# Expert products of 512 columns, gate/up one block ahead of down, in a hybrid Mamba and mixture-of-experts layer

## The reference

```
xb  = xt[tok]                                     # gather the block's tokens
gu  = xb @ w_gate_up[e] + b_gate_up[e]            # 1024 -> 2048
glu = min(gu[:, :1024], 7);  lin = clip(gu[:, 1024:], -7, 7)
act = glu * sigmoid(1.702 * glu) * (lin + 1)
yb  = (act @ w_down[e] + b_down[e]) * g[:, None]  # 1024 -> 1024
out[tok] += yb
```

## Time and profile before

| | us |
|---|---|
| median of 3 runs | 1605.25 (1603.05 to 1607.25) |
| the profiled execution | 1617.12 |
| its span, first to last instruction | 1615.5 |
| experts, first to last expert matmul | 538.4 to 1586.5 |
| TensorE busy | 1518.4 (94% of the span) |
| weight loads busy | 1282.4 (79%) |
| VectorE busy | 605.4 (37%) |
| 384 transfers of 1 MB, median from issue to landing | 12.7 |

### The profile page before, as it was taken

How to read it: one execution, slowest core, us unless ns; L and a number is a source line. 1 busy time by engine, 2 the same in 40 slices (tenths; PEclk the granted TensorE clock), 3 DMA queues, 4 the chain that set the end, 5 groups by cost and what they waited for, 6 DMA issues and landing times.

```text
span 1615.5 us, 50223 instructions
## 1 busy us (share of the span) xinstructions
PE 1518.4 (94%) x21227; PEld 1282.4 (79%) x21227; DVE 605.4 (37%) x1324; ACT 297.4 (18%) x449; POOL 380.3 (24%) x511
## 2 busy tenths in 40 slices
PE   6898999999995699999999999999999999999994
PEld 4897889875453367799989888889997898999883
DVE  4666988865024222322232222232232223232223
ACT  5442333342021001110110110011011011011102
POOL 1000000000003323233323333232324232333332
PEclk8998999999997799999999999999999999999997
DMA  3222222142446599999999999999999999999983
GB/s 117 78 79 104 105 104 104 56 178 104 197 156 178 202 404 403 398 406 406 406 397 405 404 403 397 403 401 408 402 396 407 405 402 398 407 404 408 395 310 120
DMA packets 88777, 478.79 MB, mean 296 GB/s; under 512 B 16374, under 2 KB 29178, under 8 KB 34610
## 3 DMA queue, kind: packets, MB, share of 16 engines
q1 hardware_dynamic: 65266, 456.94, 70.1%
q0 software_dynamic: 23488, 21.55, 6.7%
HBM read 463.66 MB, written 19.07 MB: 299 GB/s over the span
## 4 chain that ended last, share of the span: by engine, by line
PE 64%; issue 2%; DMA 1%; DVE 1%; POOL 0%; ACT 0%; POOLq 0%; ACTq 0%; DVEq 0%; SPq 0%
PE bank L1399 64%; DMA expert_sum<-moe_f,idx_now 0%; DMA ring<-expert_sum 0%; DMA moe_f<-n_scratch,idx_next 0%; DVE reg_x L1158 0%; DVE reg_b L1146 0%; DVE reg_b L1158 0%; DVE reg_x L1146 0%; POOL slot_table L490 0%; POOL expert_sum L524 0%; DMA idx_raw<-slot_table 0%; POOL idx_raw L504 0%; ACT reg_a L740 0%; DVE moe_f L1095 0%; ACT moe_f L733 0%
## 5 line engine op out<-in xcount | busy, mean ns | idle before, releaser
L1399 PE MATMUL bank<-ring,moe_f 128*32 128x256 f32 x18432 | 1029.9, 380 | 30.6 <-issue 17.4
L1399 PEld LDWEIGHTS bank<-ring,moe_f 128*32 128x32 f32 x18432 | 905.2, 110 | 155.3 <-issue 65.7
L1118 DVE STREAM_TRANSPOSE moe_f<-bank 128x384 f32<-128x384 f32 x64 | 37.3, 583 | 659.1 <-PE bank L1399 635.7
L524 POOL DMA_INDIRECT expert_sum<-moe_f,idx_now x96 | 154.1, 1606 | 341.8 <-ACT moe_f L733 311.4
L1171 PE MATMUL bank<-n_hi,w_hi 128*128 128x264 f32 (+2 forms) x640 | 199.4, 312 | 6.4 <-DVE w_lo L775 5.9
L1171 PE MATMUL bank<-n_lo,w_hi 128*128 128x264 f32 (+2 forms) x640 | 196.5, 307 | 0.0
L1171 PE MATMUL bank<-n_hi,w_lo 128*128 128x264 f32 (+2 forms) x640 | 196.2, 307 | 0.0
L728 ACT ACTIVATE moe_f<-moe_f 128x384 f32<-128x384 f32 x64 | 33.5, 523 | 652.9 <-DVE moe_f L1121 632.1
L1171 PEld LDWEIGHTS bank<-n_hi,w_hi 128*128 128x128 f32 x640 | 121.5, 190 | 15.3 <-issue 8.7
L1171 PEld LDWEIGHTS bank<-n_lo,w_hi 128*128 128x128 f32 x640 | 121.7, 190 | 5.7 <-issue 0.5
L1171 PEld LDWEIGHTS bank<-n_hi,w_lo 128*128 128x128 f32 x640 | 121.6, 190 | 5.5
(11 more groups left out here) (207 smaller groups left out, 848.6 us busy)
## 6 DMA issues: line engine op xcount, KB each, us to landing
ring<-in_moe SPq DMA_DIRECT2D x384, 1024.0 KB, 12.7
ring<-in_w_in SPq DMA_DIRECT2D x24, 1024.0 KB, 5.1
ring<-in_w_out SPq DMA_DIRECT2D x10, 1024.0 KB, 5.6
ring<-acs_scratch SPq DMA_DIRECT2D x4, 1024.0 KB, 6.7
idx_raw<-slot_table POOLq DMA_DIRECT2D x136, 0.8 KB, 5.4
reg_vcs<-in_xT SPq DMA_DIRECT2D x4, 528.0 KB, 6.5
reg_x<-in_xrow SPq DMA_DIRECT2D x4, 512.0 KB, 5.9
expert_sum<-reg_a SPq DMA_DIRECT2D x4, 512.0 KB, 2.8
```

What stands on the lines that cost most here:

```text
L524: g.indirect_dma_start(out=acc_parts, in_=y_sb[:, n, :], in_offset=None, out_offset=bass.IndirectOffsetOnAxis(ap=idx_now[:, 2 * n:2 * n + ...
L1118: v.transpose(glu.rearrange("p b (g r) -> p g b r", g=GRANULES), gate).then_inc(gate_raw, 1)
L1399: ins = mm(out[l * LANE:(l + 1) * LANE, g * QUARTER:(g + 1) * QUARTER], x[:, at, g * LANE:(g + 1) * LANE], w[:, l * QUARTER:(l + 1) * QUAR ...
```

## The change

Gate/up is no longer split into two halves of the features. A matmul of gate/up streams 512 columns, and a piece of gate/up is 12 matmuls; the sum of all eight pieces stands in banks 0 to 2. Down is as before. A block is now 96 + 96 = 192 matmuls.

VectorE works on the whole block at once: each transpose, the combining and the product are 768 columns wide where they were 384, and bias and clamp are 8 instructions of 96 columns for gate and 8 for up. The next tokens are transposed between the two. The result goes to one `act_t`, which VectorE may write when down of the previous block is done (`dn_used`).

TensorE runs gate/up of block j and then down of block j - 1. Ahead of the loop stands gate/up of block 0, behind it down of the last block. SyncE issues the transfers in the same order. GpSimd keeps two more index lists (`idx_kept`), since it gathers for block j + 3 while it adds the result of block j, and copies lists on at three places, not one.

```diff
-FF_HALF = 512
-FF_LANE = FF_HALF // LANES
+FF_LANE = D // LANES
...
-        bias = view(moe_f, 6144, EXPERTS * 4 * FF_BLOCKS)
-        act_h = [view(moe_f, 3712 + n * FF_BLOCKS * BLOCK, FF_BLOCKS, BLOCK) for n in range(2)]
+        bias = view(moe_f, 6144, EXPERTS * 2 * FF_BLOCKS)
+        act_t = view(moe_f, 7680, FF_BLOCKS, BLOCK)
...
+            def gate_up(j, e):
+                for q in range(GU):
+                    hold(gu_used, j * GU + (q + 1 - GU))
                     sp.dma_start(slot(q), moe_d[ds(e, 1), q].rearrange("o p w -> (o p) w")).then_inc(w_in[q], 16)
-            with sp.Fori(1, EXPERTS) as j:
-                pieces(j, j)
+            def down(j, e):
+                for q in range(GU, PIECES):
+                    hold(dn_used, j * DN + (DN + q + 1 - GU))
+                    sp.dma_start(slot(q), moe_d[ds(e, 1), q].rearrange("o p w -> (o p) w")).then_inc(w_in[q], 16)
+            for q in range(GU):
+                hold(gu_used, q + 1)
+                sp.dma_start(slot(q), moe_d[1, q]).then_inc(w_in[q], 16)
+            with sp.Fori(2, EXPERTS) as j:
+                gate_up(j, j)
+                down(j - 1, j - 1)
...
+            down(n_blocks - 1, expert_of(n_blocks - 1))
...
-            def keep_rows():
-                g.tensor_copy(now[:, :, 0], nxt[:, :, 0]).then_inc(idx_moved, 1)
-                g.tensor_copy(now[:, :, 1].bitcast(F32), nxt[:, :, 1].bitcast(F32)).then_inc(idx_moved, 1)
+            def move_rows(to, of):
+                g.tensor_copy(to[:, :, 0], of[:, :, 0]).then_inc(idx_moved, 1)
+                g.tensor_copy(to[:, :, 1].bitcast(F32), of[:, :, 1].bitcast(F32)).then_inc(idx_moved, 1)
...
-            list_rows(CAPACITY)
-            pool.wait_ge(x_in, 16 * GRANULES)
-            keep_rows()
-            pool.wait_ge(idx_moved, 4)
-            pool.wait_ge(idx_in, 32 * LANES)
+            for b in range(1, 3):
+                list_rows(b * CAPACITY)
+                pool.wait_ge(idx_in, (b + 1) * 16 * LANES)
+                pool.wait_ge(x_in, b * 16 * GRANULES)
+                pool.wait_ge(idx_moved, 4 * b)
+                lane_rows()
+                pool.wait_ge(idx_moved, 4 * b + 2)
+                pool.wait_ge(xT_ready, b)
+                gather()
+                move_rows((mid1, mid2)[b - 1], nxt)
+            list_rows(3 * CAPACITY)
+            pool.wait_ge(x_in, 3 * 16 * GRANULES)
+            pool.wait_ge(idx_moved, 12)
+            pool.wait_ge(idx_in, 4 * 16 * LANES)
             lane_rows()
-            pool.wait_ge(idx_moved, 6)
+            pool.wait_ge(idx_moved, 14)
             pool.wait_ge(h2_out, 16 * TT)
             pool.sem_inc(y_room, 1)
-            with pool.Fori(0, n_blocks) as j:
-                hold((xT_ready, j + 1))
+            with pool.Fori(0, n_blocks - 1) as j:
+                hold((xT_ready, j + 3))
                 gather()
-                base = pool.value_load(blocks[0:1, ds(2 * j + 4, 1)], min_val=0, max_val=EXPERTS * CAPACITY - BLOCK)
+                base = pool.value_load(blocks[0:1, ds(2 * j + 8, 1)], min_val=0, max_val=EXPERTS * CAPACITY - BLOCK)
                 list_rows(base)
                 hold((y_ready, j + 2))
                 scatter()
-                hold((idx_in, j * (16 * LANES) + 48 * LANES), (x_in, j * (16 * GRANULES) + 32 * GRANULES),
+                hold((idx_in, j * (16 * LANES) + 80 * LANES), (x_in, j * (16 * GRANULES) + 64 * GRANULES),
                      (y_out, j * (16 * GRANULES) + 16 * GRANULES))
-                keep_rows()
-                hold((idx_moved, j * 4 + 8))
+                move_rows(now, mid1)
+                hold((idx_moved, j * 8 + 16))
                 pool.sem_inc(y_room, 1)
+                move_rows(mid1, mid2)
+                hold((idx_moved, j * 8 + 18))
+                move_rows(mid2, nxt)
+                hold((idx_moved, j * 8 + 20))
                 lane_rows()
-                hold((idx_moved, j * 4 + 10))
+                hold((idx_moved, j * 8 + 22))
+            hold((y_ready, n_blocks + 1))
+            scatter()
...
-            with act.Fori(0, n_blocks) as j:
-                for h in range(2):
-                    act.wait_ge(glu_ready, j * 2 + h + 1)
-                    a.activation(sig, glu, ACT.Sigmoid, scale=ALPHA).then_inc(sig_ready, 1)
-                act.wait_ge(piece_used, j * PIECES + PIECES)
+            def sigmoid(j):
+                act.wait_ge(glu_ready, j + 1)
+                a.activation(sig, glu, ACT.Sigmoid, scale=ALPHA).then_inc(sig_ready, 1)
+            def evict(j):
+                act.wait_ge(dn_used, j * DN + 3 * DN)
                 act.wait_ge(y_room, j + 1)
                 y = bank[:, 4:6, :].rearrange("p a b -> p (a b)")
                 for n in range(GRANULES):
                     ins = a.activation(y_sb[:, n, :], y[:, n * QUARTER:(n + 1) * QUARTER], ACT.Copy,
                                        scale=idx_now[:, 2 * n + 1:2 * n + 2].bitcast(F32))
                 ins.then_inc(y_ready, 1)
+            sigmoid(0)
+            with act.Fori(1, n_blocks) as j:
+                sigmoid(j)
+                evict(j - 1)
+            evict(n_blocks - 1)
...
-            dve.sem_inc(gu_free, 2)
+            dve.sem_inc(gu_free, 1)
+            dve.sem_inc(act_ready, 1)
...
+                gate, lin = (bank[:, 0:GRANULES, k * FF_LANE:(k + 1) * FF_LANE].rearrange("p g (b r) -> p g b r", r=LANE)
+                             for k in range(2))
+                dve.wait_ge(gu_used, j * GU + GU)
+                dve.wait_ge(act_ready, j + 1)
+                v.transpose(glu.rearrange("p b (g r) -> p g b r", g=GRANULES), gate).then_inc(gate_raw, 1)
+                v.transpose(up.rearrange("p b (g r) -> p g b r", g=GRANULES), lin).then_inc(gu_free, 1)
+                dve.wait_ge(gate_raw, j + 1)
+                for b in range(FF_BLOCKS):
+                    ins = v.tensor_scalar(glu[:, b, :], glu[:, b, :], bias_col(0, b), LIMIT, ALU.add, ALU.min)
+                ins.then_inc(glu_ready, 1)
                 x_transposed(j + 2)
+                dve.wait_ge(gu_free, j + 2)
+                for b in range(FF_BLOCKS):
+                    ins = v.tensor_scalar(up[:, b, :], up[:, b, :], bias_col(1, b), 1.0 - LIMIT, ALU.add, ALU.max)
+                ins.then_inc(up_ready, 1)
+                dve.wait_ge(up_ready, j + 1)
+                dve.wait_ge(glu_ready, j + 1)
+                v.scalar_tensor_tensor(up, up, 1.0 + LIMIT, glu, ALU.min, ALU.mult).then_inc(lin_ready, 1)
+                dve.wait_ge(lin_ready, j + 1)
+                dve.wait_ge(sig_ready, j + 1)
+                dve.wait_ge(dn_used, j * DN + 2 * DN)
+                v.tensor_tensor(act_t, up, sig, ALU.mult).then_inc(act_ready, 1)
...
+            def lanes(first_bank, width, x, at, w, first, last):
+                out = bank[:, first_bank:first_bank - (-GRANULES * width // 512), :].rearrange("p a b -> p (a b)")
+                for g in range(GRANULES):
+                    opens = first and g * width % 512 == 0
+                    for l in range(LANES):
+                        ins = mm(out[l * LANE:(l + 1) * LANE, g * width:(g + 1) * width],
+                                 x[:, at, g * LANE:(g + 1) * LANE], w[:, l * width:(l + 1) * width],
+                                 start=opens, stop=last, skip_group_check=True)
+                return ins
+            def piece_here(j, q):
+                pe.wait_ge(w_in[q], j * 16 + 16 * (HELD[q] + 1))
+            def gate_up(j):
+                pe.wait_ge(xT_ready, j + 1)
+                pe.wait_ge(gu_free, j + 1)
+                for q in range(GU):
+                    piece_here(j, q)
+                    lanes(0, 2 * FF_LANE, xT, q, slot(q), q == 0, q == GU - 1).then_inc(gu_used, 1)
+            def down(j):
+                pe.wait_ge(act_ready, j + 2)
+                pe.wait_ge(y_ready, j + 1)
+                for q in range(GU, PIECES):
+                    piece_here(j, q)
                     for u in range(2):
-                        w = slot(q)[:, u * D:(u + 1) * D]
-                        if q < GU:
-                            h, c = q // 4, q % 4 * 2 + u
-                            ins = lanes(2 * h, xT, c, w, c == 0, c == KC - 1)
-                        else:
-                            h, c = (q - GU) // 2, (q - GU) % 2 * 2 + u
-                            ins = lanes(4, act_h[h], c, w, (h, c) == (0, 0), (h, c) == (1, FF_BLOCKS - 1))
-                    ins.then_inc(piece_used, 1)
-                pe.wait_ge(xT_ready, j + 1)
-                pe.wait_ge(gu_free, j * 2 + 1)
-                for q in range(4):
-                    piece(q)
-                pe.wait_ge(gu_free, j * 2 + 2)
-                for q in range(4, GU):
-                    piece(q)
-                pe.wait_ge(y_ready, j + 1)
-                pe.wait_ge(act_ready, j * 2 + 1)
-                piece(8)
-                piece(9)
-                pe.wait_ge(act_ready, j * 2 + 2)
-                piece(10)
```

(14 more changed lines are left out.)

61 lines of the change are left out of this document (14 added, 47 removed).

## The result

The changed kernel takes 1611.35 us (median of 5 runs, 1610.59 to 1612.98), the kernel before beside it 1605.25 (5 runs, 1603.05 to 1607.25). The ratio is 1.0038, with a 95% interval of 1.0023 to 1.0053: slower by 6.1 us. Predicted were 1611 us and +6. The profile shows that the number is right and that one of its steps is not: the gap in each block is gone, and TensorE waits for pieces instead.

What follows compares the result with a forecast made beforehand. TensorE was taken to bound the kernel, at 32.72 us a block, with the DMA engines close behind at 33.0. Terms -3 + 4.8 + 2.6 + 1.3 + 0.3 = +6.0 us on 1605.25 gave 1611 us, range 1595 to 1616.

Steps and rivals of the forecast that it cites:

- the gap: TensorE's idle time in each block, tied to GpSimd's gather and list fetch: stays within down, unchanged at 1.7 us, effect 0.
- I carry the difference over unchanged: The profiled execution is 11.9 us above the median of the runs; the same difference was assumed after the change.
- signs of being wrong: Blocks of 31 us, missing gaps, and TensorE waiting for pieces (landings near 28 us) from the middle on.
- rival 1: In the blocks, the gap shrinks and the DMA engines bind at 33.0 us a block: -9 us, 1596 us; chance 0.20.
- Columns: Gate/up in 192 records of 512 columns instead of 384 saves 0.1 us a block: -3 us over 32 blocks.
- Start: Gate/up of block 1 waits for VectorE behind block 0's: +4.8 us, and the clock falls in that pause: +2.6 us.
- End: Last down waits for VectorE's product and two semaphores, +1.3 us; ScalarE waits for room in `y_sb`, +0.3 us.
- Rival 2: In the blocks, the gap is an instruction fetch that goes with the loop body's length; gone or halved, 1596 us; chance 0.05.
- Rival 4: On TensorE, the loads of weights were the limit after all: 1596 us; chance 0.03.
- Rival 3: In the blocks or at the end, a transfer is late: +5 to +10, 1613 to 1618 us; chance 0.10 together with Rival 5.
- Rival 5: In gate/up, 512 columns do not go in one record: +9, 1614 us; chance 0.10 together with Rival 3.

Runs made afterwards that it cites:

- e9: The changed kernel without the pause at the start: gate/up of block 0 reads its tokens elsewhere and sums into banks 5 to 7; 1605.03 us, 0.9995 of before.
- e8: The kernel before without the gathers in the loop, every block working on the first block's tokens, list fetches kept; 1571.61 us, 0.9742 of before.
- e6: The changed kernel with all index lists fetched ahead of the loop instead of in each block; 1611.94 us, 0.9995 of before.
- e5: The changed kernel run and profiled again in a later series, no edit; 1614.20 us, 1.0008 of before.
- e2: The kernel before with only half of every piece transferred from the second block on; 1601.33 us, 0.9928 of the unedited kernel before.
- e7: The kernel before with all index lists fetched ahead of the loop instead of in each block; 1608.99 us, 0.9970 of the unedited kernel before.

## Why the prediction was right, and where it was not

**Two kinds of execution.** The profile that the prediction was read from (1617.1) showed a gap in each block. The timed runs that it had to forecast had none, as far as can be told: the changed kernel's profile has none, and before takes 1605.2 in both series where after or its variants show none, against 1612.6 to 1613.7 in the three others, where every kernel with gathers shows one. Within a series the kind never changed, so it goes with the chip or with something else that holds for a series; no chip was used in two series, which leaves this open. On which chip the first profile was taken is not known. No profile of before without the gap was taken, so that before too is bound by the DMA engines there is argued and not shown. What e9 says of it: its 363rd of the 372 pieces behind the first block's (piece 6 of the last block) is there at 1547.2; before needs 9 pieces more, at 33.04 / 12 us each, and 2.7 us for the last: 1574.7. With the 30.6 us from the last expert matmul to the end of the execution (1617.1 - 1586.5) that is an estimate of 1605.3, and 1605.2 was measured.

**The step that failed** is "I take it as unchanged, 1.7 us in each of 31 blocks: 0" (the gap), with "I carry the difference over unchanged". The prediction's own signs of being wrong all came: blocks of 31 us, gaps that are missing, TensorE waiting for pieces, landings of 29 us. The 11.9 us between profile and median were a hint that the timed runs had another bound. What held in its place is the bound of rival 1, DMA engines at 33.0 us a block (33.05 measured), but not its price: -9 was taken against a kernel before with its gap. If before is bound by the DMA engines as well, nothing is gained in the steady state.

**Columns:** -0.1 us a block was forecast. Without a gap, a block takes 31.08 us before (e8, without gathers and on another chip) and 30.96 after: -0.12, 3.8 us in all. Right.

**The gap where it exists:** 1.52 us before (32.60 - 31.08), 1.44 after (32.40 - 30.96). Unchanged but for 0.08, 2.5 us in all; the times are from different chips, so this is rough. That it goes with GpSimd and not with TensorE's program was right; the gather is needed for it and the list fetch has nearly no part (e6 to e8).

**Start:** +4.8 and +2.6. The pause was 4.44, the clock fell in it and was back before 570, and e9 prices both at 6.9 us. Right, and for a reason that the argument did not have: it counts though the DMA engines bind. Where the gap is, the pause is there too (4.45 us in e5), but no run prices it there.

**End:** +1.3 and +0.3; 1.5 measured, with the copies of ScalarE beside the product.

**The sum** under each bound. With the gap: -3.8 for the columns, -2.5 for the gap, +6.9 for the start and +1.5 for the end make +2.1 us; measured was +1.4 (e5, not told from none). Without it: +6.9 for the start, and a rest of -0.8 to the measured +6.1; columns and gap are worth nothing, since the DMA engines set the pace. So that +6 came out is in part luck. The start was priced rightly. But the prediction set it against a kernel with its gap, and with a gap in each block, the case that it describes, the change costs 1.4 us and not 6; the 6 came where the gap was missing and the two gains don't count.

**The rivals.** Rival 2: the gap is no fetch of instructions in TensorE's body. The Trainium skill, "Runtime: NRT & Kernel Launch", section "Instruction fetch mechanics", would have it with the loop's body; e8 has the body of before and no gap. And in e5, with a gap in each block, two packets of instructions are seen from 600 to 1580 us. Rival 4: the loads of the same kernel are busy 378.6 us in one profile and 594.5 in another (e5), and columns cost the same. In before they are busy 8.41 of the 15 us from 575 (288 records, ahead of the first gap) and 9.50 of the 10 us from 600 (192 records, behind it), at the same pace of records, so their busy share follows the gap and does not cause it: the busy share that "Trainium Kernel Development and Optimization", section "Performance Expectations", of the Trainium skill recommends as a measure says nothing here. Rival 3: the last piece was 0.4 us late, no more. Rival 5: 192 records of 512 columns, it did what it says.

**What stays open:** why gathers starve TensorE, and why in some series only. With half the load on the DMA engines 1.1 of the 1.5 us stay in before (32.17 - 31.08, e2), and without the list fetches 1.4 (e7), so neither is the main cause.

## What to carry to other kernels

A profiled execution that is far from the median of the timed runs may have another bound, so both bounds have to be summed before the difference is carried over. A pause at the start of a streamed stretch can cost its full length even where the transfers bind later on, since the full ring stops them too (7 us of transfers here). Idle transfer time at the end costs nothing if the engine has its own work behind the last awaited piece. Where an engine is starved while GpSimd gathers, try to put the gathers apart; here this is likely to have helped, and it ran only together with other edits.

## What was not expected of the hardware

The same program takes 31.0 us a block in one series and 32.4 in another. And SyncE's issue itself takes longer when the DMA engines are far behind. Early in after, one transfer's issue took 0.33 us (first row); in its chain of waits, with landings at 29 us, each of the others is one transfer's issue:

```profile
624.11 0.33 SPq L417 DMA_DIRECT2D ring<-in_moe  x1
```

```profile
1046.49 2.46 SPq L411
...
1049.27 4.03 SPq L411
...
1053.63 1.92 SPq L411
```
